# Placing the gate's quarter tiles in the decode of stick-breaking attention: fewer among the key steps, more among the value steps

## Chip, cores and metric

One core of a Trainium2 chip runs the whole program in one launch. The metric is the device time of that launch in microseconds, as the median of several runs. Times inside the program come from one profiled execution.

## What is computed

The kernel is one inference step of a hybrid decoder with two layers: 512 prompt tokens and 32 sample tokens (8 sequences of 4), all in f32. Each layer projects the normed input, runs three branches (RWKV-7 time mixing, stick-breaking attention, dilated windows), gates each with a silu of its own projection, and merges them. Two parts of the reference meet in the stretch of this case. The first is the decode of the stick-breaking branch, in which 4 new tokens of each sequence attend to 1024 cached positions held in 8 pages of 128:

```
past_k = cache_b_k[l][page_table].reshape(bs, past, B_HEADS, HEAD_DIM)
past_v = cache_b_v[l][page_table].reshape(bs, past, B_HEADS, HEAD_DIM)
...
z = einsum('bqhd,bkhd->bhqk', q, k_all) * HEAD_DIM ** -0.5 + bias
log_beta = log_sigmoid(z)
log_rest = where(before, log_beta - z, 0.0)
later = cumsum(log_rest, reverse=True) - log_rest
w = where(before, exp(log_beta + later), 0.0)
y = einsum('bhqk,bkhd->bqhd', w, v_all)
```

The second is the gate of branch A, which has nothing to do with the first and is spread among its steps:

```
ya = ya * silu(za)          # za = (xn @ w_in)[:, columns of za], 512 columns
```

## The kernel before

**The stage.** `stage_stick_breaking` has three blocks for each layer: the projection of q, k and v, the attention of the prompt, and the decode. The change is in the decode, the block whose instructions stand on the lines 1750 to 1955. In the trace it lies at 599 to 705 us (layer 1) and 2007 to 2113 us (layer 2); both layers run the same instructions.

**Key steps.** The 8 sequences are handled in two halves of four. A step takes one page number of the four sequences of one half: 16 steps (`NCH`), of which 1 to 8 are half 0 and 9 to 16 are half 1. For each, TensorE turns four tiles (`turn_keys`, L1791, 16 transposes in four rounds, each into one of three PSUM banks), ScalarE and VectorE copy the rounds to `k_pages_t` in turn (L1761, even rounds on ScalarE and odd ones on VectorE), and TensorE multiplies the queries with them (L1831, 32 small products). The transposes of step n+1 are issued ahead of the scores of step n. A round waits until the round three before it was copied.

**From scores to weights.** After the eighth step VectorE adds the bias (`scores_of`, L1927), ScalarE does abs, exp and ln (`logs_of`, L1871 to L1875; each change of function loads a table), VectorE adds, scans and subtracts (`rests_of`, L1936 to L1942), and ScalarE takes the exp (`weights_of`, L1879). For half 0 these instructions are placed between the copies of steps 10 to 15, for half 1 they come behind step 16 and run beside the first half's value steps.

**Value steps.** `turn_weights(half)` turns the weights (L1791, on `dzb`), then eight pages of values are multiplied with them (L1850, eight products for a page). In half 0, `turn_weights(1)` comes after the sixth page. `own_rows` and `own_heads` (L1953, L1815) pick each head's part out, and the stage ends with those of half 1.

**Loads.** Each load is one page of four sequences, 4 x 256 KB, into one of 7 slots (`load_pages`, L1419). Loads 0 to 15 are keys, 16 to 31 values. SyncE issues them strictly in order; loads 0 to 5 were issued in the blocks before. Load m waits until slot m % 7 is free: for the transposes of load m - 7 if that is a page of keys, for the products of it if it is a page of values. For loads 7 to 21 SyncE also reads the four page numbers first.

**The gate's quarters.** The gate's projection has four tiles of 128 channels. A tile is 48 products (three for each of eight k-tiles and two halves of the tokens, L428), and `tile_quarter` issues 12 of them. `Quarters` places the 16 quarters, in order, at numbered places: 0 ahead of everything, 1 to 16 between the transposes of the next step and the scores of this one, 17 after the first half's weights are turned, 18 to 25 after each value page of half 0, 26 ahead of half 1, 27 to 34 after each of its pages. The lists hold how many quarters stand at each place. All tiles use one pair of PSUM banks, so a tile's first quarter waits for the evacuation of the tile before. Where a tile ends, ScalarE runs `gate_silu` (L1743, wait for the tile, table load, silu; then one load of 512 KB for a later chunk of weights from its own queue, L286, and the high parts of the next weights, L381), and VectorE runs `gate_branch` (L1751, then the low parts, L391). Both are called for a place by `gate_silus` and `gate_branches`, at fixed points of the two instruction streams:

```python
for i in range(0, NKR, 2):
    ...
    if i % 4 == 0 and i >= 8:
        gate_silus(i // 4 - 1, i // 4)
    take(a, a.copy, i, takeA)
...
gate_silus(VALUES[0], VALUES[0] + 3)
weights_of(1)
gate_silus(VALUES[0] + 3, VALUES[0] + 2 + TURN_AFTER_VALUES)
take(a, a.copy, NKR + 4, takeA)
```

Of the kernel before, what the change touches and what calls it, by code (L numbers as in the profile page):

```python
# [1375 lines left out]
def stage_stick_breaking(nc, c, e):  # L1376
# [332 lines left out]
    NK = PAST_LEN + NDEC  # L1709
    g0, g1 = PLAN["gate_a"]  # L1710
    split = e.Split(list(range(g0, g1)), c2, P, "gate_a")
    FIRST, IN_KEYS = 0, [0, 1] * 4 + [1, 0, 1, 0, 1, 0, 0, 1]
    TURN, IN_VALUES = 3, [1, 0, 0, 0, 0, 0, 0, 0] + [0] + [1, 0, 1, 0, 1, 0, 1, 0]
    tiles = e.Quarters(split, [FIRST] + IN_KEYS + [TURN] + IN_VALUES)
    VALUES = (1 + NCH, 2 + NCH + N_PAGES)
    TURN_AFTER_VALUES, OWN_AFTER_VALUES = 5, 1
# [1070 lines left out]


STAGES = [stage_norm, stage_rwkv, stage_stick_breaking, stage_windows, stage_output]


# [32 lines left out]
```

## Time and profile before

| | us |
|---|---|
| median of 3 runs | 2824.67 (2823.83 to 2824.96) |
| the profiled execution | 2825.71 |
| its span | 2824.1 |
| TensorE busy in it | 2502.8 (89%) |
| VectorE busy | 1257.9 (45%) |
| ScalarE busy | 913.9 (32%) |
| GpSimd busy | 185.8 (7%) |
| the decode blocks of this case, layers 1 and 2 | 599 to 705, 2007 to 2113 |

Over the span the DMA engines moved 345.53 MB, 122 GB/s on average. A busy share says how much of the span an engine worked, not whether the work around it waited for it; for the stretch of this case the rows below are by windows and by instruction. PE is TensorE, PEld its weight loads, DVE VectorE, ACT ScalarE, SP SyncE; a q behind an engine's name is its sequencer, which issues transfers.

### The profile page before, as it was taken

How to read it: one execution, taken by the hardware profiler on the slowest of the kernel's cores; microseconds unless marked ns; L12 is line 12 of the kernel's file. 1: busy time of each engine (PE TensorE's matmuls, PEld its weight loads, DVE VectorE, ACT ScalarE, POOL GpSimd, SP SyncE). 2: the span in 40 equal slices, each digit the busy share in tenths (PEclk: the TensorE clock that was granted, in tenths of full speed). 3: DMA queues.
4: the chain of work that ended last, by engine and by line, in shares of the span. 5: the costliest groups of instructions: out<-in, count | busy, mean ns of one | idle time of the engine just before them, and what ended most of it. 6: DMA issues, size and time to landing. Idle time of an engine off the chain costs nothing. (4 is left out here: it accounts for less than half of the span.)

```text
span 2824.1 us, 57983 instructions
## 1 busy us (share of the span) xinstructions
PE 2502.8 (89%) x24330; PEld 2239.7 (79%) x24330; DVE 1257.9 (45%) x1932; ACT 913.9 (32%) x1404; POOL 185.8 (7%) x276
## 2 busy tenths in 40 slices
PE   3978989898999689999959789898989996899998
PEld 3868879675999477999958689796759985769998
DVE  4554443343666543333344644423436665433333
ACT  1432012444333443322124320124443334432221
POOL 0012110110011000000000121101101110000000
PEclk9989779999999899999979897799999998999999
DMA  4200613248223159565232006122482230686561
GB/s 142 75 17 4 218 47 101 77 124 295 71 81 91 34 129 261 187 220 200 83 120 62 18 4 221 56 91 74 146 273 79 84 95 19 156 234 224 190 229 63
DMA packets 267506, 345.53 MB, mean 122 GB/s; under 512 B 32116, under 2 KB 225878, under 8 KB 265656
## 3 DMA queue, kind: packets, MB, share of 16 engines
q1 hardware_dynamic: 245384, 328.13, 36.8%
q10 hardware_dynamic: 21856, 13.63, 1.8%
q8 instruction: 194, 3.18, 0.5%
q14 instruction: 72, 0.59, 0.1%
HBM read 322.65 MB, written 102.68 MB: 151 GB/s over the span
## 5 line engine op out<-in xcount | busy, mean ns | idle before, releaser
L411 PE MATMUL ps<-x_hi,w_hi 128*128 128x272 f32 x2304 | 685.8, 298 | 47.3 <-DVE w_lo L391 40.6
L411 PE MATMUL ps<-x_hi,w_lo 128*128 128x272 f32 x2304 | 676.7, 294 | 0.0
L411 PE MATMUL ps<-x_lo,w_hi 128*128 128x272 f32 x2304 | 675.5, 293 | 0.0
L411 PEld LDWEIGHTS ps<-x_hi,w_hi 128*128 128x128 f32 x2304 | 446.4, 194 | 59.0 <-issue 36.6
L391 DVE TENSOR_TENSOR w_lo<-ring,w_hi 128x1024 fp32r<-128x1024 f32 (+4 forms) x194 | 254.5, 1327 | 466.4 <-ACT w_hi L381 445.2
L411 PEld LDWEIGHTS ps<-x_lo,w_hi 128*128 128x128 f32 x2304 | 446.5, 194 | 0.9
L411 PEld LDWEIGHTS ps<-x_hi,w_lo 128*128 128x128 f32 x2304 | 445.6, 193 | 0.0
L381 ACT CAST w_hi<-ring 128x1024 fp32r<-128x1024 f32 (+4 forms) x194 | 214.1, 1126 | 174.1 <-PE ps L447 62.6
L460 PE MATMUL ps<-w_hi,x_hi 128*128 128x256 f32 (+1 forms) x480 | 137.0, 286 | 13.7 <-DVE x_lo L2777 13.7
L460 PE MATMUL ps<-w_hi,x_lo 128*128 128x256 f32 (+1 forms) x480 | 137.4, 286 | 0.0
L460 PE MATMUL ps<-w_lo,x_hi 128*128 128x256 f32 (+1 forms) x480 | 136.4, 284 | 0.0
L2189 DVE RECIPROCAL c_squared<-c_squared 128x544 f32<-128x544 f32 x36 | 127.7, 3547 | 3.1 <-ACT c_squared L2150 3.1
L999 POOL TENSOR_TENSOR inv_lm<-inv_lt,levels 128x256 f32<-128x256 f32 (+1 forms) x82 | 59.7, 754 | 980.9 <-DVE inv_lt L1054 909.4
L428 PE MATMUL ps<-x_hi,w_hi 128*128 128x272 f32 x352 | 108.9, 309 | 7.6 <-DVE w_lo L391 3.9
L2725 ACT ACTIVATE gate<-ps 128x544 f32<-128x544 f32 x48 | 30.0, 625 | 244.3 <-PE ps L411 244.2
L428 PE MATMUL ps<-x_hi,w_lo 128*128 128x272 f32 x352 | 102.0, 290 | 0.0
L428 PE MATMUL ps<-x_lo,w_hi 128*128 128x272 f32 x352 | 101.9, 289 | 0.0
L447 PE MATMUL ps<-y_hi,w_hi 128*128 128x272 f32 x352 | 101.3, 288 | 0.0
L447 PE MATMUL ps<-y_hi,w_lo 128*128 128x272 f32 x352 | 101.2, 287 | 0.0
L447 PE MATMUL ps<-y_lo,w_hi 128*128 128x272 f32 x352 | 100.9, 287 | 0.0
L460 PEld LDWEIGHTS ps<-w_hi,x_hi 128*128 128x128 f32 (+1 forms) x480 | 85.1, 177 | 14.6 <-DVE w_lo L391 14.1
L2202 POOL TENSOR_TENSOR c_raw<-c_raw,rot_cos 128x544 f32<-128x544 f32 x36 | 48.7, 1352 | 597.6 <-PE ps L2098 597.6
(383 smaller groups left out, 4583.4 us busy)
## 6 DMA issues: line engine op xcount, KB each, us to landing
ring<-in_w_in_dram SPq DMA_DIRECT2D x44, 1024.0 KB, 5.4
ring<-in_w_in_dram SPq DMA_DIRECT2D x62, 512.0 KB, 4.2
c_rows<-in_cache_c_kv_dram SPq DMA_DIRECT2D x40, 768.0 KB, 13.7
out_c_kv_sample_dram<-in_cache_c_kv_dram SPq DMA_DIRECT2D x16, 1524.0 KB, 17.0
pages_early<-in_cache_b_k_dram SPq DMA_DIRECT2D x80, 256.0 KB, 3.8
pages_early<-in_cache_b_v_dram SPq DMA_DIRECT2D x80, 256.0 KB, 5.7
c_rows<-in_cache_c_kv_dram SPq DMA_DIRECT2D x32, 384.0 KB, 10.1
pages_more<-in_cache_b_k_dram SPq DMA_DIRECT2D x32, 256.0 KB, 3.8
```

The costliest lines, as they stand in the source:

```text
L381: a.copy(self.w[0][:, i % 2, k, 0:w], weights(a, n)[:, k, 0:w]).then_inc(self.w_hi, 1)
L391: v.tensor_tensor(self.w[1][:, i % 2, k, 0:w], weights(v, n)[:, k, 0:w], hi, ALU.subtract).then_inc(self.w_lo, 1)
L411: last = pe.matmul(o[:, half, 0:HALF], self.w[w][:, i % 2, k, c * P:(c + 1) * P], self.x[x][:, k, half * HALF:(half + 1) * HALF], start=(k ...
L428: last = pe.matmul(ps[:, half, 0:HALF], self.w[w][:, i % 2, k, c * P:(c + 1) * P], self.x[x][:, k, half * HALF:(half + 1) * HALF], start=( ...
L447: last = pe.matmul(o[:, half, 0:HALF], self.w[w][:, i % 2, k, c * P:(c + 1) * P], y[x][:, k0 + k, half * HALF:(half + 1) * HALF], start=(k ...
L460: last = pe.matmul(o[0:m, 0, 0:CHUNKS[n][2]], self.x[x][:, k, t0:t0 + m], self.w[w][:, i % 2, k, 0:CHUNKS[n][2]], start=(k == 0 and j == 0 ...
L999: g.tensor_tensor(lm[0:m, :].rearrange("p (i t) -> p i t", t=c), lt[0:m, :].rearrange("p (i t) -> p i t", t=c), mk, ALU.mult).then_inc(poo ...
L2189: v.reciprocal(r[:, :], r[:, :]).then_inc(sin_done, 1)
L2202: g.tensor_tensor(x[:, :], x[:, :], cos[:, :], ALU.mult).then_inc(cos_done, 1)
L2725: a.activation(halves(gate[:, u % 2]), e.pair(u)[:, :, 0:HALF], func).then_inc(e.products_taken[u % 2], 1)
```

## The change

Two lists of counts change. The sum stays 16, place 0 and place 17 keep 0 and 3 quarters, and half 1 keeps its four.

```diff
-    FIRST, IN_KEYS = 0, [0, 1] * 4 + [1, 0, 1, 0, 1, 0, 0, 1]
-    TURN, IN_VALUES = 3, [1, 0, 0, 0, 0, 0, 0, 0] + [0] + [1, 0, 1, 0, 1, 0, 1, 0]
+    FIRST, IN_KEYS = 0, [0] * 8 + [2, 0, 0, 0, 0, 0, 2, 0]
+    TURN, IN_VALUES = 3, [1, 0, 1, 1, 1, 1, 0, 0] + [0] + [1, 0, 1, 0, 1, 0, 1, 0]
```

| place | 2 | 4 | 6 | 8 | 9 | 11 | 13 | 15 | 16 | 17 | 18 | 20 | 21 | 22 | 23 | 27 to 34 |
|---|---|---|---|---|---|---|---|---|---|---|---|---|---|---|---|---|
| before | 1 | 1 | 1 | 1 | 1 | 1 | 1 | 0 | 1 | 3 | 1 | 0 | 0 | 0 | 0 | 4 |
| after | 0 | 0 | 0 | 0 | 2 | 0 | 0 | 2 | 0 | 3 | 1 | 1 | 1 | 1 | 1 | 4 |

The tiles end at other places by this: tile 0 at place 15 instead of 8, tile 1 at 18 instead of 16, tile 2 at 23 instead of 18, tile 3 at 33 in both.

## Rows read from the trace of the kernel before

**Rows 1.** By window: length; PE, PEld, DVE, ACT, POOL busy; PEclk; DMA share; GB/s.
```profile
665.00:670.00 5.00, 5.00 (x40) 4.01 (x40) 1.93 (x3) 4.94 (x6) 0.00 (x0) 1.00 1.05 369
670.00:675.00 5.00, 5.00 (x46) 2.16 (x48) 3.98 (x4) 4.07 (x4) 0.00 (x0) 1.00 0.85 277
675.00:680.00 5.00, 3.13 (x33) 1.34 (x25) 2.79 (x5) 1.67 (x2) 0.00 (x0) 1.00 1.07 373
680.00:697.00 17.00, 13.78 (x108) 6.73 (x100) 0.69 (x1) 0.21 (x1) 0.00 (x0) 1.00 1.05 386
2073.00:2078.00 5.00, 5.00 (x41) 4.01 (x40) 2.21 (x3) 4.95 (x6) 0.00 (x0) 1.00 0.77 247
2078.00:2083.00 5.00, 5.00 (x48) 2.44 (x50) 3.74 (x3) 4.34 (x5) 0.00 (x0) 1.00 0.78 238
```

**Rows 2.** TensorE in order of time: start us, us, what, idle before and releaser.
```profile
635.50 1.08 PE L1831 MATMUL ps<-k_pages_t,bq_blocks 128*32 128x128 f32 x32 [0.43 <-DVEq L1929]
...
642.46 0.66 PE L1791 MATMUL ps<-ident,pages_more 128*128 128x128 f32 x4 [1.49 <-ACT k_pages_t L1761]
...
668.43 1.07 PE L1850 MATMUL ps<-pages_early,d_weights_t 128*32 128x512 f32 x8
671.12 1.06 PE L1850 MATMUL ps<-pages_early,d_weights_t 128*32 128x512 f32 x8
...
673.72 1.04 PE L1850 MATMUL ps<-pages_late,d_weights_t 128*32 128x512 f32 x8
...
677.49 1.20 PE L1791 MATMUL ps<-ident,dzb 128*128 128x128 f32 x9 [1.87 <-ACT dzb L1879]
...
681.46 1.06 PE L1850 MATMUL ps<-pages_early,dsp 128*32 128x512 f32 x8
...
697.58 1.07 PE L1850 MATMUL ps<-pages_early,dsp 128*32 128x512 f32 x8 [1.65 <-DMA pages_early<-in_cache_b_v_dram]
700.28 1.07 PE L1850 MATMUL ps<-pages_early,dsp 128*32 128x512 f32 x8
...
2089.74 1.07 PE L1850 MATMUL ps<-pages_early,dsp 128*32 128x512 f32 x8
...
2107.74 1.06 PE L1850 MATMUL ps<-pages_early,dsp 128*32 128x512 f32 x8
```

**Rows 3.** Waits of SyncE's queue, layer 1 then 2: total us, times, longest.
```profile
SPq L1419 <- PE ps L1850: 3.3, 1, 3.3
...
SPq L1419 <- PE ps L1850: 7.5, 3, 6.1
```

**Rows 4.** Loads 6 and 13, 22, 23: ns min/median/max, first and last start us.
```profile
L1419 SPq DMA_DIRECT2D pages_late<-in_cache_b_k_dram x8: 337/338/372, 600.7 to 630.8; - x8
...
L1419 SPq DMA_DIRECT2D pages_early<-in_cache_b_v_dram x4: 381/418/614, 664.0 to 665.8; - x4
...
L1419 SPq DMA_DIRECT2D pages_early<-in_cache_b_v_dram x4: 332/382/1344, 669.6 to 671.9; - x4
```

**Rows 5.** Transposes of key steps 3, 4 and 5 on TensorE.
```profile
609.20 1.99 PE L1791 MATMUL ps<-ident,pages_early 128*128 128x128 f32 x16
...
612.12 1.99 PE L1791 MATMUL ps<-ident,pages_more 128*128 128x128 f32 x16
...
616.56 1.99 PE L1791 MATMUL ps<-ident,pages_more 128*128 128x128 f32 x16
```

**Rows 6.** Windows again: the first key steps, layer 2's first transposes, the next stage.
```profile
599.00:606.50 7.50, 6.79 (x80) 5.93 (x81) 6.11 (x13) 5.16 (x11) 0.00 (x0) 1.00 0.51 150
...
1441.00:1444.90 3.90, 3.67 (x16) 3.27 (x16) 3.87 (x7) 0.00 (x0) 0.00 (x0) 0.50 0.02 6
1445.00:1448.00 3.00, 2.13 (x16) 1.72 (x16) 2.90 (x3) 2.11 (x2) 0.00 (x0) 1.00 0.00 0
...
707.50:711.00 3.50, 3.50 (x16) 3.50 (x17) 2.02 (x4) 1.20 (x2) 0.00 (x0) 0.50 0.06 5
```

**Rows 7.** ScalarE: the silu of tile 1, layer 1.
```profile
672.56 0.62 ACT L1743 ACTIVATE gate_a<-ps 128x544 f32<-128x544 f32 x1
```

## The prediction, made blind

> **What bounds the kernel now.** I started with the page: TensorE is the busiest engine, and the chain of work that ended last gives its lines no share that would single out this stage, so I read the stage in windows. In the decode part of stick breaking (599 to 705 us in layer 1, 2007 to 2113 in layer 2) TensorE is not what decides the end. From 670 us on the sixteen DMA engines are [rows 1]: the windows show 373 to 386 GB/s at a DMA share of 1.05 or more, while TensorE is idle for a fifth of the time from 680 to 697. I take 387 GB/s as their ceiling, 1 above the mean of the 17 us from 680 on. The last value pages confirm it: TensorE starts them after waits of 1.65 us for a transfer, 2.70 us apart [rows 2]. A slot holds four pages of 256 KB, 1.05 MB, and 1.05 MB at 387 GB/s is 2.71 us. So the second half's value steps run at the pace of the loads, and the stage ends when the last load has landed and its products are done.
>
> Why are the transfers late? The rows show two holes just before that stretch: 277 GB/s from 670 to 675 us in layer 1, and 247 and 238 GB/s from 2073 to 2083 in layer 2 [rows 1]. They have one origin. SyncE issues the loads in order; load 23 needs the slot of value page 0 and waits for its products, once for 3.3 us in layer 1 and once for up to 6.1 us in layer 2 [rows 3]. Load 22 was issued from 664.0 and load 23 only from 669.6 us [rows 4], right behind the start of page 0's products at 668.43 [rows 2]. The loads before it (7 to 22) never waited for TensorE in either layer: the rows of waits name no other wait of SyncE for products. Their pace is SyncE's own: it reads four page numbers and issues four transfers. Loads 6 and 13 go to the same slot, the first starts at 600.7 and the second's last transfer at 630.8 [rows 4]; less the 1.8 us by which a load's last transfer starts behind its first (664.0 to 665.8) that is 28.3 us for 7 loads, 4.0 us each.
>
> **The change.** It adds and removes no instruction. In steps 1 to 8 of the keys four quarters go; steps 9 to 16 keep four, but as two pairs (before the scores of page 8 and of page 14); the first half's value steps get five where one stood (four of them added). The gate tiles so end later: tile 0 after step 15 and not after 8, tile 1 still at the first value page, tile 2 at its sixth page and not its first. Moved with them are the evacuation on ScalarE, the product and the low-part subtraction on VectorE, and one weight load of 512 KB issued from ScalarE's queue for each tile. SyncE's own queue is moved past by nothing.
>
> *Keys, steps 1 to 8.* Transposes to transposes take 609.20 to 612.12, 2.92 us, without a quarter, and 612.12 to 616.56, 4.44 us, with one [rows 5]: a quarter is worth 1.5 us. Four leave: -6.0 us. The copies out of PSUM (two on ScalarE, two on VectorE for a step) keep up in the steps that have no quarter today, so I charge nothing for them.
>
> *Keys, steps 9 to 16.* The pair in step 9 covers the wait of 0.43 us for the first half's scores [rows 2], which then goes. The exp, ln, scan and weight steps of the first half run on ScalarE and VectorE between the copies; the wait of 1.49 us [rows 2] stays, and with no quarters in steps 10 to 14 behind it two more open up: following the copies in order with their durations gives 0.8 us in step 12 (the copy behind the ln) and 0.9 us in step 14 (the copy behind the scan). Sum at value page 0: -6.0 - 0.4 + 1.7 - 0.4 (small waits that shrink), less rounding, -5.3 us. Page 0 starts at 663.1 and not at 668.43.
>
> *First half's values.* A page with a quarter behind it takes 668.43 to 671.12, 2.69 us, and one without 0.87 (three from 671.12 to 673.72) [rows 2]. Four more quarters are 4 x 1.82 = +7.3 us. Against that, the 1.87 us for which TensorE waits today before it turns the second half's weights [rows 2] goes, since exp, ln and scan now run under the added quarters. New is the first quarter of tile 2: it needs tile 1 out of PSUM, and today tile 1's last product is followed by page 1's at 671.12 [rows 2], and its activation ends at 672.56 + 0.62 = 673.18 [rows 7], 2.0 us later (a table load stands ahead of it). The pages 1 and 2 cover 1.8 of it: +0.2. TensorE so reaches the second half's first page at 681.46 - 5.3 + 7.3 - 1.9 + 0.2, that is 681.6 to 681.8 us: nothing gained on TensorE, and this is the point of the case. VectorE then has tile 2's product in front of the last two copies that this page needs; by my times these end 0.2 us before they are wanted.
>
> *Transfers.* Here is the gain. Page 0's products end 5.3 us earlier, so load 23 need not wait: 3.3 us go in layer 1, about 5.3 of 6.1 in layer 2. Loads 24 to 31 follow pages that end before SyncE comes to them or while at least two loads stand queued, so the engines stay fed. What the end gains are the missing bytes. Layer 1: 5 us x ((387-369) + (387-277) + (387-373))/387 = 1.8 us. Layer 2: 5 x ((387-247) + (387-238))/387 = 3.7 us. The weight load of tile 0 moves from 630 us into the stretch at 655 to 660, where the engines have room; those of tiles 1 and 2 stay inside the full stretch, so its bytes are as before.
>
> *Who ends last then.* From 681.7 TensorE needs 4 x 2.70 + 2 x 0.87 + 1.99 = 14.5 us to the last page's products if it never waits, so 696.2. Today these start at 700.28 in layer 1 and, less the 1408.3 us between the layers (2089.74 against 681.46), at 699.4 in layer 2 [rows 2]. TensorE thus allows 4.1 and 3.2 us. Layer 1 gains min(1.8, 4.1) = 1.8, layer 2 min(3.7, 3.2) = 3.2. The sum is -5.0 us. The profiled execution took 2825.71 us (span 2824.1, 1.6 around it), 1.0 above the median of 2824.67; the steps are worth the same in either, so 2819.7.
>
> *The clock.* Steps 1 to 8 become 24 us of nothing but transposes and narrow products. Today's longest such stretch, 599 to 606.5, ran at a granted clock of 1.00, the level of 2.4 GHz [rows 6]. The layer's first transposes are harder evidence: sixteen of them, with no other work on TensorE, ran at 0.50 (1.2 GHz) up to 1444.9, and the next ones at 1.00 [rows 6]. So transposes alone raised the clock. The Trainium skill says otherwise (TensorE: Matmul & The Clock Gate, Part 4: PE-mode transpose): in its words "HAM K=8/8 doesn't engage for transpose-mode". By that rule the bare steps fall to 1.2 GHz and the change loses; the trace speaks against it, and I give the rule a small chance as the second rival.
>
> **The rivals.** (a) *The transfers end no earlier.* If the engines cannot hold 387 GB/s from 666 us on, because the queue isn't deep enough while SyncE still issues one load behind each page, or if tile 1's weight load, now in the middle of it, takes the room, the last load lands within 1 us of today: 2823.7 to 2824.7. For it: a load that stands nearly alone lands at a slower pace than 2.71 us (windows at 277 GB/s with a share of 0.85). Against it: the window 665 to 670 has 369 GB/s with only loads 21 and 22 under way.
>
> (b) *The clock falls in the bare key steps.* The end is slower then. Sixteen transposes took 3.67 us at 0.50 and 2.13 at 1.00 [rows 6], +1.5 us a step; if the 32 score products (1.08 us today) double too, +1.0 more, so up to 2.5 us a step. TensorE can be later than forecast by 4.1 us in layer 1 and 3.2 in layer 2 before the stage ends later than today, so the change turns into a loss once about one and a half steps in each layer run at half clock; all eight would cost 8 x 2.5 = 20 a layer, less 4.1 and 3.2: 2 x 20 - 7.3 = +33 us, 2858. Two steps a layer give 2 x 5 - 7.3 = +2.7, 2827; four give 2837.
>
> (c) *More is gained.* If SyncE's loads 7 to 22 meet fewer slow issues in layer 1, as they do in layer 2, both layers end at TensorE's own pace: -4.1 - 3.2 = -7.3 us, 2817.4.
>
> **How the numbers follow.** My forecast (a gain of 2 to 7 us, both layers) has 0.60, (a) 0.20, (b) 0.07, (c) or more 0.13. What stands behind the stage adds scatter to each: the products of the next stage run at half clock from 707.5 to 711 [rows 6], which is worth half of that stretch, so where it falls can move either layer by about 1.7 us. The unknown waits (0.8, 0.9 and 0.2 us above) move TensorE by up to 2 us, which layer 2 feels. The range therefore is 2815.5 to 2825.0: below it (c) with lucky clocks, above it (b). A measurement of this kernel tells 0.2%, 5.6 us, from no change. My 5.0 lies just inside: faster gets 0.28 of my 0.60 and 0.12 from (c), 0.40; slower 0.06, nearly all of (b); the same 0.54.
>
> **What would show it.** Right: SyncE's waits for value products fall below 1 us in layer 1; load 23 is issued near 666 us; no window from 667 us on is under 360 GB/s in layer 1; page 0 starts at 663 us; TensorE no longer waits before the second half's weights; the last page starts near 698.5 and 2104.5. Wrong: a granted clock of 0.50 between 607 and 627 us; a wait of TensorE for tile 1's evacuation above 1 us; the last load landing at 700 again, which would mean that the ceiling isn't bytes but SyncE's order; or loads 7 to 22 issued later than today.

## The result and the profile after

Nine runs of the changed kernel gave a median of 2816.97 us (2812.09 to 2822.38), nine of the kernel before 2824.67 us. The ratio is 0.9974 with a 95% interval of 0.9963 to 0.9986. A second measurement on another occasion (e1 below, twelve runs) gave 2820.24 us and 0.9985, interval 0.9976 to 0.9993. By the medians the change saves 7.7 us in the first measurement and 4.1 in the second; the forecast was 5.0.

The profiled execution of the changed kernel took 2822.38 us, the slowest of its nine runs, so its stage shows less than the median does. I give times in the stage from its first transposes (row one below; they began at 599.16 us in the kernel before).

TensorE in order of time in the changed kernel, layer 1 (start us, us, what, idle before and releaser):

```profile
598.57 1.50 PE L1791 MATMUL ps<-ident,pages_early 128*128 128x128 f32 x12 [0.93 <-PEq L1578]
...
659.90 1.06 PE L1850 MATMUL ps<-pages_early,d_weights_t 128*32 128x512 f32 x8
...
687.82 1.06 PE L1850 MATMUL ps<-pages_late,dsp 128*32 128x512 f32 x8 [0.98 <-DMA pages_late<-in_cache_b_v_dram]
690.54 1.94 PE L1850 MATMUL ps<-pages_early,dsp 128*32 128x512 f32 x8 [1.66 <-DMA pages_early<-in_cache_b_v_dram]
695.42 2.60 PE L1850 MATMUL ps<-pages_early,dsp 128*32 128x512 f32 x16
699.65 1.07 PE L1850 MATMUL ps<-pages_early,dsp 128*32 128x512 f32 x8
702.53 1.07 PE L1815 MATMUL ps<-rowtoken,d_own_head 128*128 128x16 f32 x8 [0.81 <-DVE d_own_head L1953]
```

Value page 0 starts 659.90 - 598.57 = 61.3 us into the stage, against 668.43 - 599.16 = 69.3 before [rows 2]. The wait of 1.87 us ahead of the second half's weights is gone, and so is the one of 1.49 us in key step 12. The last page starts at 101.1, where before it was 700.28 - 599.16 = 101.1 too. In layer 2 it is 100.1 against 100.2. The heads' products end the stage 1.0 us earlier in layer 1 and 0.8 us in layer 2. The transfers do end earlier in this profile too: the last of the loads lands 100.0 us into the stage in both layers, against 101.0 and 100.2 before (from the semaphore events of the traces).

SyncE's waits for products in the changed kernel, layer 1 and then layer 2 (total us, times, longest):

```profile
SPq L1419 <- PE ps L1850: 0.5, 2, 0.4
...
SPq L1419 <- PE ps L1850: 0.4, 1, 0.4
```

They were 3.3 and 7.5 us [rows 3]. Load 23 follows:

```profile
L1419 SPq DMA_DIRECT2D pages_early<-in_cache_b_v_dram x4: 379/604/946, 665.6 to 668.0; - x4
```

Windows of the changed kernel: length, busy time of PE, PEld, DVE, ACT and POOL, granted clock, DMA share, GB/s:

```profile
607.00:627.00 20.00, 20.00 (x346) 17.58 (x339) 9.20 (x14) 8.07 (x14) 0.00 (x0) 1.00 0.84 265
665.00:670.00 5.00, 5.00 (x40) 3.20 (x39) 3.91 (x5) 2.96 (x3) 0.00 (x0) 1.00 1.03 343
670.00:675.00 5.00, 5.00 (x41) 3.84 (x38) 0.00 (x0) 0.29 (x1) 0.00 (x0) 1.00 1.05 383
675.00:680.00 5.00, 5.00 (x43) 1.68 (x42) 2.20 (x4) 2.10 (x3) 0.00 (x0) 1.00 1.06 382
...
680.00:685.00 5.00, 4.10 (x34) 2.22 (x32) 0.00 (x0) 0.21 (x1) 0.00 (x0) 1.00 1.10 359
...
690.00:697.00 7.00, 6.46 (x30) 3.38 (x34) 0.00 (x0) 0.00 (x0) 0.00 (x0) 0.51 0.94 346
```

The hole of 277 GB/s at 670 to 675 [rows 1] is filled to 383. (The 359 GB/s of the row from 680 are taken up below.) The bare key steps, 607 to 627, ran at a granted clock of 1.00. The last row shows something else: from 690 to 697 TensorE ran at half clock, behind waits of 0.98 and 1.66 us for loads. The last load landed at 100.0 us, but TensorE, still catching up, came to its page only at 101.1, without a wait for it. So the half clock hid about 1 us of the gain in layer 1 of this profile. In layer 2 it fell as well, but earlier, and the last page (100.1) starts right behind the landing (100.0): it cost nothing there.

ScalarE during the first half's abs, exp and ln, changed kernel:

```profile
632.09 1.09 ACT L1871 ACTIVATE dsp<-dzb 128x1056 f32<-128x1056 f32 x1
633.21 0.58 ACT L1761 COPY k_pages_t<-ps 128x512 f32<-128x512 f32 x1
633.69 1.09 ACT L1873 ACTIVATE dsp<-dsp 128x1056 f32<-128x1056 f32 x1
634.81 0.58 ACT L1761 COPY k_pages_t<-ps 128x512 f32<-128x512 f32 x1
635.29 1.09 ACT L1875 ACTIVATE dsp<-dsp 128x1056 f32<-128x1056 f32 x1
```

and the same place in the kernel before:

```profile
639.41 1.28 ACT L1873 ACT_TABLE_LOAD   x1
640.70 1.08 ACT L1873 ACTIVATE dsp<-dsp 128x1056 f32<-128x1056 f32 x1
641.82 0.58 ACT L1761 COPY k_pages_t<-ps 128x512 f32<-128x512 f32 x1
642.42 1.28 ACT L1875 ACT_TABLE_LOAD   x1
```

Exp and ln need no table load any more. Tile 0's silu used to stand ahead of them at key step 8 and now comes behind them, so the table of the prompt's attention (which does exp and ln too, with no load between 540 and 600 us) is still loaded. So not every change of function loads a table, as I had written of `logs_of`. Over the stage a layer loads a table 6 times and not 10: three loads go with tile 0's silu (exp, ln and the exp of the weights, first half), and one goes with tile 2's, which moves behind the second half's exp, so that the last silu finds its table loaded. The Trainium skill names the cause: in "ScalarE: Activation LUTs", section "Table sets: the hidden batching unit", one set holds exp and ln together, while functions of different sets cost a load at each change. The trace agrees, at 1.28 us a load, with one thing beside it: with a silu ahead of them, exp and ln cost a load each (the rows of the kernel before), so exp's load there brought a table that ln could not use. I had not counted any of this.

### The profile page after: what moved, and what is told of

Same layout as the page of the kernel before. It is cut to its first block and busy times, and to the rows that moved or that the text cites. A ratio compares the mean times of both kernels' runs of the same rounds, so it can differ in the third digit from the quotient of the medians.

```text
span 2820.8 us, 57975 instructions
## 1 busy us (share of the span) xinstructions
PE 2507.6 (89%) x24330; PEld 2239.9 (79%) x24330; DVE 1257.8 (45%) x1932; ACT 903.7 (32%) x1396; POOL 185.8 (7%) x276
## 5 line engine op out<-in xcount | busy, mean ns | idle before, releaser
L411 PEld LDWEIGHTS ps<-x_hi,w_hi 128*128 128x128 f32 x2304 | 446.1, 194 | 59.7 <-issue 36.6
L999 POOL TENSOR_TENSOR inv_lm<-inv_lt,levels 128x256 f32<-128x256 f32 (+1 forms) x82 | 59.7, 754 | 976.7 <-DVE inv_lt L1054 906.9
L428 PEld LDWEIGHTS ps<-x_hi,w_hi 128*128 128x128 f32 x352 | 68.4, 194 | 34.2 <-issue 34.1
```

What stands on the lines that cost most here:

```text
L411: last = pe.matmul(o[:, half, 0:HALF], self.w[w][:, i % 2, k, c * P:(c + 1) * P], self.x[x][:, k, half * HALF:(half + 1) * HALF], start=(k ...
L428: last = pe.matmul(ps[:, half, 0:HALF], self.w[w][:, i % 2, k, c * P:(c + 1) * P], self.x[x][:, k, half * HALF:(half + 1) * HALF], start=( ...
L999: g.tensor_tensor(lm[0:m, :].rearrange("p (i t) -> p i t", t=c), lt[0:m, :].rearrange("p (i t) -> p i t", t=c), mk, ALU.mult).then_inc(poo ...
```

## The experiments

All compare with the kernel before on the same chip: e1 to e4 on one chip (35 runs of the kernel before), e5 to e8 on another (29). Each kernel ran twelve times, e8 six times. The changed kernel ran with the first group only, so e5, e6 and e8 are set beside it across two chips, whose medians of the kernel before were 2824.34 and 2824.65 us.

**e1, the change again.** No edit.

> The changed kernel once more, to stand beside the others of this group on one chip. Theory 1 (transfers: with value page 0 done 5 us earlier, SyncE no longer waits before load 23 and the last load lands earlier, 2 to 3 us in a layer) and theory 2 (only the stage's last links changed: ScalarE's silu of tile 2 now comes behind the exp of the second half's weights, so the last silu needs no table load) both expect what was measured, 4 to 10 us less than the kernel before. SyncE's waits for value products are under 1 us a layer.

Measured: 2820.24 us, ratio 0.9985 (0.9976 to 0.9993). In its profile page 0 starts at 61.4 us again, and the last page at 97.7 (layer 1) and 96.7 (layer 2), 3.4 us earlier than in the profile above, for the same kernel. Its stage never ran at half clock before the last page, and SyncE came to load 22 at 62.1 and 61.4 us, against 64.1 and 64.4 in that profile.

**e2, half of the move.**

```diff
-    FIRST, IN_KEYS = 0, [0] * 8 + [2, 0, 0, 0, 0, 0, 2, 0]
-    TURN, IN_VALUES = 3, [1, 0, 1, 1, 1, 1, 0, 0] + ...
+    FIRST, IN_KEYS = 0, [0] * 8 + [2, 0, 1, 0, 1, 0, 2, 0]
+    TURN, IN_VALUES = 3, [1, 0, 1, 0, 1, 0, 0, 0] + ...
```

> Half of the move: two quarters instead of four leave the key steps for the value steps (steps 1 to 8 are empty as in the change, the quarters of steps 11 and 13 stay). Theory 1: value page 0 is done about 3 us earlier than before instead of 5.3, which is most of SyncE's 3.3 us of layer 1 and half of the 6 us of layer 2; 3 to 5 us less than before. Theory 2: tile 2 still ends behind the exp, so all of the gain stays, as much as in the full change. A third view, that the empty steps 1 to 8 alone matter, also expects the full gain.

Measured: 2825.62 us, ratio 1.0008 (0.9998 to 1.0018), no gain. The count was right and the boundary was not: with six quarters in the keys, the three at place 17 run into tile 2, and its first quarter waits for tile 1's silu, which ScalarE does behind the second half's exp and ln. TensorE's row, and SyncE's waits:

```profile
666.59 0.56 PE L428 MATMUL ps<-x_hi,w_hi 128*128 128x272 f32 x1 [4.12 <-ACT gate_a L1743]
```

```profile
SPq L1419 <- PE ps L1850: 8.8, 2, 7.7
```

Page 0 started at 69.8 us, as late as before the change, although the first eight steps are as empty as in the change and tile 2 ends behind the exp. So neither theory 2 nor the view that the empty steps are enough holds. That the time of page 0 counts fits, but this run doesn't isolate it. As the wait of 4.12 us ended the granted clock was down: 0.52 from 665 to 672 us, which is a part of page 0's delay.

**e3, the order of silu and exp alone,** in the kernel before.

```diff
-            gate_silus(VALUES[0], VALUES[0] + 3)
             weights_of(1)
-            gate_silus(VALUES[0] + 3, VALUES[0] + 2 + TURN_AFTER_VALUES)
+            gate_silus(VALUES[0], VALUES[0] + 2 + TURN_AFTER_VALUES)
```

> The kernel before with one thing of the change alone: ScalarE runs the silu of tile 2 behind the exp of the second half's weights, as it falls out in the change; no quarter moves. Theory 1: the quarter lists give nearly all of the gain, so this one is worth only the last links: the end waits for the later of silu and product of tile 3 (1.28 us earlier without the load) and the last page's products, so about 0.65 us a layer, 1.3 in all, 2823. Theory 2: all of the gain, 7 us, is here.

Measured: 2824.86 us, ratio 0.9999 (0.9989 to 1.0010). From the last page's products to the end of the heads' products it takes 3.9 us in both layers, against 4.9 and 4.5 before: the last links are shorter by 0.6 to 1.0 us, as in the change. But the last pages start at 102.6 and 102.1 us, later than before (101.1 and 100.2); whether the new order costs something there or it is chance, this run doesn't tell. The interval reaches from -3.1 to +2.8 us, so the 1.3 us that were expected can't be told from nothing, but 7 us can: theory 2 falls.

**e4, load 23 held back,** in the changed kernel. This one changes nothing but the release of the loads.

```diff
                 if used >= NCH:
-                    sp.wait_ge(y_mm, used - NCH + 1)
+                    sp.wait_ge(y_mm, max(used - NCH + 1, 5))
```

> The changed kernel, but SyncE issues loads 23 to 27 only when the fifth value page of the first half is done (wait for 5 products instead of 1 to 4), about 4.6 us later than in the change and about 1 us later than before. Everything on TensorE, ScalarE and VectorE is placed as in the change. Theory 1: the hole before the full stretch is back and the last load lands as before or 1 us later, so the time is that of the kernel before within 3 us, and 5 to 9 us above the change. Theory 2: no change, it is as fast as the change, since the order of the functions on ScalarE is the change's.

Measured: 2824.30 us, ratio 0.9999 (0.9990 to 1.0007); the whole gain is gone. TensorE reaches page 0 at 61.3 us as in the change, and the second half at 80.2, 0.4 later, behind a wait for a load. SyncE waits 8.5 us, and the hole is back, deeper than before. Its window:

```profile
670.00:675.00 5.00, 5.00 (x40) 3.06 (x38) 1.16 (x2) 0.51 (x1) 0.00 (x0) 1.00 0.27 92
```

The hold went too far: load 23 goes at 71.7 us, 1.3 later than before, and the last pages start at 102.3 and 101.9, 1.2 and 1.6 later than before, which the shorter end makes up for in part. So this run shows that the release of load 23 decides (4.1 us against e1, on the same chip); it does not measure what the release alone is worth.

**e5, the other four key quarters kept.**

```diff
-    FIRST, IN_KEYS = 0, [0] * 8 + [2, 0, 0, 0, 0, 0, 2, 0]
+    FIRST, IN_KEYS = 0, [0, 1] * 4 + [0] * 8
```

> The same move with the other four key quarters kept: the key steps 2, 4, 6 and 8 keep theirs as before and steps 9 to 16 are left empty; the value steps are those of the change. Tile 0 ends at step 8 again, so its silu stands ahead of the first half's exp and the table loads before exp, ln and the weights' exp are back (3 of 1.28 us a layer). Theory A (what counts is when value page 0 is done, and the table loads only count as far as they delay it): TensorE waits more in steps 12 to 15 since no quarter covers exp and ln; page 0 starts at about 64 us from the stage's first transposes against 61.3 in the change and 69.3 before, load 23 is issued at 66, and the time is at most 2 us above the change. Theory B (the empty first eight steps count, since loads free their slots earlier there): the gain is gone, 2824.

Measured: 2819.23 us, ratio 0.9985 (0.9974 to 0.9997), the same as e1. Page 0 starts at 66.3 us and not at 64: TensorE waits 1.9 us for the first half's scores, 3.0 for ScalarE's copies and 1.2 for VectorE's. Even so load 23 is issued at 67.5, against 70.4 before. Which key steps are emptied does not matter beyond that; theory B falls.

**e6, the table loads back,** in the changed kernel.

```diff
+                if i == 4 * 10 - 2:
+                    a.activation(scratch[:, :], K["ident"][:, 0:1], ACT.Silu)
                 if 4 * 10 <= i < 4 * 10 + 6:
                     logs_of(0, i // 2 - 20)
```

(`scratch` is a column of its own, added above.)

> The changed kernel with one more silu of a single column on ScalarE ahead of the first half's abs, exp and ln, so that the table loads which the change lost there are back; the quarters stand as in the change. It adds a silu that nobody reads. Value page 0 then starts about 2.6 us later (64 against 61.3) and the second half's first page at 82.4 against 79.8. Theory 1 (transfers): load 22 is issued at 62 to 64 anyway and load 23 at most 1 us later than in the change, so no more than 1.5 us in all is lost. Rival (the table loads are the gain): 4 to 5 us are lost, 2824.

Measured: 2820.49 us, ratio 0.9977 (0.9966 to 0.9988). ScalarE's table loads are there again:

```profile
637.05 1.28 ACT L1873 ACT_TABLE_LOAD   x1
640.07 1.28 ACT L1875 ACT_TABLE_LOAD   x1
650.87 1.28 ACT L1879 ACT_TABLE_LOAD   x1
```

Page 0 moves to 64.3 and the second half to 82.7 us, 2.9 later than in the change, load 23 still goes at 65.5 us (66.1 in the changed kernel's profile), and nothing is lost that can be told. The loads of tables explain why TensorE was earlier than I forecast, and they are not the gain. These two times are those of my forecast for the change (64.0 and 82.5), which had kept the table loads, within 0.3 us.

**e7 and e8, page numbers read early,** in the kernel before and in the changed one. SyncE reads the numbers of loads 6 to 13 in the block ahead.

```diff
             for m in range(4, 6):
                 load_pages(sp, m, page_numbers(m))
+            for m in range(6, 14):
+                numbers[m] = page_numbers(m)
             sp.wait_ge(k_done, 5)
```

> The kernel before, with the page numbers of loads 6 to 13 read in the block ahead of the decode, where SyncE idles; loads 7 to 13 cost SyncE four issues of 0.57 us each and no reads, so load 22 is issued some 8 us earlier. Quarters as before. Theory 1: load 23 still waits for value page 0 (at 69.3 us), the wait only grows from 3 to 10 us, and the last load lands as before, 100 us: the time stays within 2 us of the kernel before. Rival (SyncE's pace is the bound in both kernels): 4 us or more are gained.

> The changed kernel with the same reads ahead of the decode. Theory 1: load 23 is now bound by page 0 (62.4 us) and not by SyncE (66), so the full stretch begins earlier and TensorE's own pace decides the end: the last page's products start at 94.4 us against 97 to 101 in the change, 2.5 to 5 us a layer, 2813 to 2816. Rival (the last loads go at the DMA engines' ceiling whatever stands before, or the ceiling falls with more in flight): no change, 2820.

Measured: e7 2823.09 us, ratio 0.9995 (0.9983 to 1.0008); e8 2809.68 us, ratio 0.9941 (0.9923 to 0.9959). With the same edit the old placing gains nothing that can be told. The new one is 15 us under the kernel before, some 10 of them beyond the change itself (2819 to 2820 in e5, e6 and e1), and 3 us under the lower end of what I expected. In e7 load 22 is out at 59.7 us, 5.1 and 1.7 earlier than in the two layers before, but load 23 still goes at 70.4: SyncE stands and waits for page 0. In e8 load 23 goes at 62.5. SyncE's waits in e7 and then in e8 (the new lines shift L1419 to L1420 and L1850 to L1852):

```profile
SPq L1420 <- PE ps L1852: 10.2, 3, 8.8
```

```profile
SPq L1420 <- PE ps L1852: 8.1, 4, 4.6
```

The end of e8's stage on TensorE has no wait for a load left (the stage began at 598.12, so the last page starts at 94.5 us, and the forecast by TensorE's own pace was 94.4; the last load lands at 94.4, just as TensorE comes to it):

```profile
688.94 2.02 PE L1852 MATMUL ps<-pages_early,dsp 128*32 128x512 f32 x16
692.59 1.07 PE L1852 MATMUL ps<-pages_early,dsp 128*32 128x512 f32 x8
```

The heads' products end 98.5 us into the stage in both layers, against 106.0 and 104.8 before: 13.8 of the 15 us.

## Why the prediction was right, point by point

- *What bounds the stage: the transfers, and among them SyncE's wait ahead of load 23.* Shown from both sides: e4 puts the wait back and loses all of the gain with everything else in place, and e8 makes the loads earlier still, until they land as fast as TensorE comes to them. One reading was loose: the full rate begins at 675 us and not at 670, since 670 to 675 is the hole [rows 1].
- *Steps 1 to 8, -6.0 us.* Right. Three of the four quarters stand ahead of step 9's transposes, which start at 621.75 - 598.57 = 23.2 us in the changed trace and at 626.85 - 599.16 = 27.7 before: 4.5 us, 3 x 1.5. No wait for copies arose.
- *Steps 9 to 16.* The term was mis-sized. I kept the wait of 1.49 us and added 0.8 and 0.9, following copies in order. The first two stood behind table loads that the change removes, and did not come. The third, behind the scan, came with 0.98 us (ahead of the fifteenth step's transposes; the prediction counts its steps 12 and 14 from zero). TensorE waited 1.5 us for copies in the whole stage, and page 0 came at 61.3 and not at 64.0. My terms also add up to -5.1 and not to -5.3. The error was harmless, since SyncE comes to load 23 only at 64 (e1) to 66 us: e6 moves page 0 back to 64.3 for nothing.
- *First half's values.* Right in size: from page 0 to the second half 18.5 us, where I had 18.6. The wait for tile 1's evacuation was 0.3 us, 0.2 expected.
- *TensorE gains nothing up to the second half.* It gained 2.5 us by the table loads, at 79.8 against 82.3, and spent them waiting for loads. So the limits that I took from TensorE's pace, 4.1 and 3.2 us a layer, were too low: in e8 the last pages start 6.6 and 5.7 us earlier than before.
- *The sum, 1.8 and 3.2 us.* Its total of 5.0 lies between the two measurements, -7.7 and -4.1, but its parts did not come out one by one, so that the total fits is partly luck. The last load landed 1.0 and 0.2 us earlier than before in the changed kernel's profile, and 3.4 and 3.5 us earlier in e1's (97.6 and 96.6 us). The division by layer rested on SyncE's times in one execution, which do not repeat: load 22 went at 64.9 and 61.4 us in the two layers before, and at 64.1 and 64.4 in the changed profile. That profile's last pages moved by 0.2 us a layer at most, e1's by 3.4 and 3.5. I left out the shorter end, 0.6 to 1.0 us a layer, since the last silu needs no table load. And I took the weight load of tile 2 to change nothing. Before, ScalarE issued it at 671.5 us, into the hole; in the change it goes at 674.9 and is under way until 687.5, and in that time the rate falls to 359 GB/s (680 to 685; also 359 at this place in e1 and e8). An estimate from these rows is 5 us x 28/387 = 0.4 us a layer; no run isolates it.
- *The rivals.* (a) fell as a whole: the measured time is below its range, and by e4 the time of load 23 decides. A part of it was true, with the weight load of tile 2 and not of tile 1. (b) fell: the clock stayed at 1.00 through the bare steps, in every profile of a kernel that has them. (c), both layers at TensorE's pace, needed SyncE's reads out of the way, and then gave more than the 7.3 us, since TensorE was 2.5 us a layer earlier than I thought and the stage's last links were shorter.
- *What I named as signs.* Load 23 at 665.6 us (near 666 named), no wait ahead of the second half's weights, SyncE's waits under 1 us: all there. That no window from 667 on would be under 360 GB/s holds to within 1 GB/s (359 from 680 to 685), up to the last bytes at 696 us. Page 0 came 2.6 us earlier than the 663 named. The last pages, named near 698.5 and 2104.5 us (99.3 and 97.0 into the stage), came at 101.1 and 100.1 in this profile and at 97.7 and 96.7 in e1's: this sign was missed in the first and passed in the second.

Open is how much of the difference between the two measurements, -7.7 and -4.1, is chance; their intervals overlap. The half clock among the last value pages is there in both layers of the changed kernel's profile, of e4's and of e7's and in layer 1 of e3's, and absent in e1, the same code as the changed kernel. It made the last page late, by 1 us, only in the first layer of the changed kernel's profile and of e3's; everywhere else the last page starts 0.1 us behind the landing of its load. Why it comes in one execution and not in another stays open.

## What to carry to other kernels

Filler work belongs where the bound resource does not depend on it. Here the order of loads hung on one release, the first value page, and every quarter placed ahead of it delayed the transfers, while a quarter behind it cost nothing that could be told, as long as TensorE stood waiting for loads later on. Ask of each placing which release it stands in front of, and who issues transfers on it. When two limits lie close (TensorE's arrival, SyncE's pace), an edit to one looks worthless until the other has moved: the same lines gained nothing in the kernel before (e7) and some ten microseconds in the changed one (e8).

## What the runs showed that I had not expected

- SyncE's pace over the first key loads is set by its own instructions: with the page numbers read inside the loop loads 7 and 8 go 3.7 us apart (603.88 and 607.58 us in the changed kernel), with the numbers at hand 2.3 (602.55 and 604.86 in e7).
- ScalarE keeps a table over blocks: moving one silu behind the first half's exp and ln took 3 of 10 loads a layer away, 1.28 us each, and moving another behind the second half's took the fourth (in e3, where only that one moves, 9 are left).
- TensorE's granted clock fell to 0.50 where it alternates between short products and waits for loads of 0.9 to 1.7 us (690 to 697 us above), although 20 us of transposes and narrow products without a pause kept it at 1.00.
